# One engine fewer for the low halves: VectorE takes over GpSimd's weight pieces in the attention stages

## The chip, the cores and the metric

The kernel runs on one core of one Trainium2 chip. Times are device microseconds (us) of one execution. The time before is the median of three runs. The profile is of one further execution, whose own time is given beside its span. The engines are called TensorE (PE in the profile, with its weight loads as PEld), VectorE (DVE), ScalarE (ACT), GpSimd (POOL) and SyncE (SP); SPq is SyncE's queue, from which all DMAs of this kernel are issued in program order.

## The reference, cut to what matters

Two layers of a hybrid attention block (each with a global attention A, a neighbourhood attention B, and gates), then one block of feed-forward, mixer, feed-forward and embedding stages, all on 272 or 256 tokens with 1024 channels in float32.

```python
proj = jnp.einsum('bld,de->ble', rms_norm(x, norm_g), w_in)
qa, ka, va, za, qb, kb, vb, zb, ga, gb = split_cols(proj)
oa = gqa_attention(rope(qa), rope(ka), va) * jax.nn.silu(za)
ob = neighbourhood_attention(qb, kb, vb, rpb) * jax.nn.silu(zb)   # scores + bias from rpb
mixed = jax.nn.sigmoid(ga) * (oa @ w_o_attn) + jax.nn.sigmoid(gb) * (ob @ w_o_na)
x = x + mixed @ w_out
```

`rpb` is the relative bias of attention B: it is gathered into a tile for each pair of heads and each tile of 128 queries.

## The kernel before, in words

**Weights in two halves.** A float32 product is made from three products of reduced-precision halves: x_hi·w_hi, x_lo·w_hi and x_hi·w_lo. The weights come as units, one DMA each. A unit of a layer has 16 blocks of 128 x 128 (1 MB). It lands in one of 3 `raw` buffers, ScalarE makes `w_hi` of it in one instruction of 128 x 2048 (`cut_to`, L798), and `w_lo = raw - w_hi` is made in 4 pieces of 128 x 512. `w_hi` and `w_lo` have 3 buffers each too. TensorE then multiplies its lines (L1946): a line is one output tile of 128 channels, 8 blocks and 24 matmuls. A unit has two such lines. The units of `ya` and `yb` have four lines of 4 blocks and 12 matmuls.

**Who makes w_lo.** `by_pool(u)` says whether the unit's name stands in `POOLS`. If it does, GpSimd makes the four pieces (L781). It does nothing else in these stages, so it makes them as soon as `w_hi` is there. If not, VectorE makes them (`lo_to`, L1227), in an order written out by hand: after it has read line g of the program out of PSUM, `lo_after` makes all pieces up to those that line g + 3 needs. Both raise a semaphore of their own, `lo_pool` or `lo_cut`. TensorE waits for it ahead of a line. SyncE waits for the last piece of unit u - 3 before it issues the load of unit u into the same `raw` buffer:

```python
if u >= RAW:
    sp.wait_ge(lo_pool if by_pool(u - RAW) else lo_cut, MADE[LO_END[u - RAW] - 1])
sp.dma_start(raw[:, u % RAW, 0:n], weights[u, :, 0:n]).then_inc(raw_in[u % RAW], 16)
```

**The attention stage of a layer.** It is a list of jobs, one per step t. ("A", c, half, t) and ("B", c, half, t) are scores of one head for 128 queries; layer 0 has 35 jobs (three of them for the 16 meta tokens), layer 1 has 32. The products that need no attention result are used as fillers between them: za (4 lines), zb (4), ga (8), gb (8), and last ya (8). Some steps have no filler: 3, 7 and 11 in layer 1, and 3, 7, 11, 15, 19 and 23 in layer 0. At step t TensorE does: scores(t), the filler's line, the turn (transpose of the probabilities) of job t-1, the values of job t-2, and, every other step, the transpose of a finished pair. VectorE does at step t: maxes(t), the filler's evacuation (L1286, L1447), the normalization of job t-2 (L1435, L1436), then `lo_after`, then the rest. ScalarE does exps(t), `cut_to` of the unit two after the filler's, the gate's tanh, and the copy of the turn of job t-1.

**The bias tiles.** The 8 bias tiles of a layer (numbered 0 to 7) share 4 `rel` buffers. `window_bias(k)` (L1376) is VectorE's first use of tile k, ahead of the maxes of a step. It waits for `rel_in`, that is for the tile's four DMAs (L700). The first four tiles are loaded early. Tiles 4 to 7 are issued by SyncE right behind a weight load:

```python
for n in range(RING, len(BIASES)):
    if u == rel_unit(i, n):
        load_rel(i, n)
```

`rel_unit` gives, in units counted from the layer's first: layer 0, tiles 4 and 5 behind the load of unit 22, 6 behind 23, 7 behind 24; layer 1, tile 4 behind 21, 5 behind 22, 6 behind 23, 7 behind 24. The load of unit 22 waits for the last low piece of unit 19, and so on. VectorE needs them at these steps: layer 0, tiles 4, 5, 6, 7 at steps 25, 27, 29, 31; layer 1 at steps 22, 24, 26, 28. Units 17 to 20 are the lines of gb, 21 and 22 those of ya, 23 and 24 those of yb.

Of the kernel before, what the change touches and what calls it, by code (L numbers as in the profile page):

```python
# [139 lines left out]

POOLS = {"za", "zb", "ga", "gb", "ya", "gv", "iq", "gr", "ms", "yg"}


def by_pool(u):

    return UNITS[u][0][1] in POOLS

# [2348 lines left out]
```

## Time and profile before

| what | value |
|---|---|
| median of 3 runs | 1212.04 us (1210.35 to 1213.66) |
| the profiled execution: time, span | 1213.4 us, 1211.6 us |
| TensorE matmul busy | 1157.0 us, 95% |
| VectorE busy | 841.1 us, 69% |
| ScalarE busy | 602.8 us, 50% |
| GpSimd busy | 263.1 us, 22% |
| HBM read | 185.50 MB |

The busy shares are averages over stages. TensorE is at work nearly all the time; each us in which it stands still, or works at the lower of its two clocks, is close to a us of the kernel's time. Outside the span lie 1.8 us of the execution's time.

### The profile page before, as it was taken

The page shows a single profiled execution, that of the slowest core. Times are in us where ns is not written, and L with a number is a line of the kernel's source. Part 1 is how long each engine was busy: PE and PEld are TensorE (multiplying, and loading weights), DVE is VectorE, ACT ScalarE, POOL GpSimd, SP SyncE. Part 2 cuts the span into 40 slices and gives each one's busy share as a digit, 9 for nine tenths or more (in the row PEclk, how much of TensorE's full clock was granted, in tenths as well). Part 3 has the DMA queues.
Part 4 walks back from the last instruction along what each step waited for, and adds up shares of the span by engine and source line. Part 5 has one row for each costly group of instructions (what it writes and reads, how often), then busy time and mean ns, then how long its engine had stood idle before and what let it go on. Part 6 is the DMA issues. An engine that isn't in the chain of part 4 may idle for free.

```text
span 1211.6 us, 23199 instructions
## 1 busy us (share of the span) xinstructions
PE 1157.0 (95%) x9292; PEld 1126.0 (93%) x9292; DVE 841.1 (69%) x1823; ACT 602.8 (50%) x940; POOL 263.1 (22%) x199
## 2 busy tenths in 40 slices
PE   6999999899999999999999989999999999999995
PEld 6989999899899998899999988888899999999995
DVE  6954444879444468787766789677855887777666
ACT  6454545453555546544444533565454564444453
POOL 1055543000655600000000058800372000000000
PEclk9999999999999999999999999999999999999998
DMA  6752343356523624555455533325454555554551
GB/s 239 181 193 106 105 126 85 140 175 166 182 105 109 168 73 174 192 201 183 168 178 180 207 140 105 140 71 168 159 134 150 177 182 194 188 176 166 191 199 35
DMA packets 47979, 188.07 MB, mean 155 GB/s; under 512 B 20856, under 2 KB 24184, under 8 KB 29312
## 3 DMA queue, kind: packets, MB, share of 16 engines
q1 hardware_dynamic: 47872, 186.58, 46.2%
q8 instruction: 75, 1.23, 0.4%
q14 instruction: 32, 0.26, 0.1%
HBM read 185.50 MB, written 1.06 MB: 154 GB/s over the span
## 4 chain that ended last, share of the span: by engine, by line
PE 76%; DVE 15%; ACT 4%; issue 2%; DMA 2%; POOL 0%; SPq 0%; DVEq 0%; ACTq 0%
PE line L1946 48%; PE result L1946 17%; DVE w_lo L1227 4%; PE turn L2072 1%; PE result L2106 1%; PE stat L2106 1%; PE score L2049 1%; ACT w_hi L798 1%; PE score L2053 1%; DMA raw<-in_weights 1%; DMA rel<-in_rpb 1%; PE score L2238 1%; DVE prod L1792 1%; DVE prod L1503 0%; DVE root L1249 0%
## 5 line engine op out<-in xcount | busy, mean ns | idle before, releaser
L781 POOL TENSOR_TENSOR w_lo<-raw,w_hi 128x512 fp32r<-128x512 f32 x184 | 258.9, 1439 | 592.0 <-ACT w_hi L798 591.9
L798 ACT ACTIVATE w_hi<-raw 128x2048 fp32r<-128x2048 f32 (+2 forms) x178 | 321.8, 1809 | 113.9 <-PE line L1946 42.3
L1946 PE MATMUL line<-x_hi,w_hi 128*128 128x256 f32 (+1 forms) x1144 | 339.1, 296 | 17.6 <-DVE x_lo L1270 8.6
L1227 DVE TENSOR_TENSOR w_lo<-raw,w_hi 128x512 fp32r<-128x512 f32 (+2 forms) x528 | 324.8, 660 | 5.5 <-ACT w_hi L798 3.0
L1946 PE MATMUL line<-x_hi,w_lo 128*128 128x256 f32 (+1 forms) x1144 | 327.1, 286 | 0.0
L1946 PE MATMUL line<-x_lo,w_hi 128*128 128x256 f32 (+1 forms) x1144 | 326.6, 285 | 0.0
L1946 PEld LDWEIGHTS line<-x_hi,w_hi 128*128 128x128 f32 x1144 | 218.5, 191 | 24.5 <-issue 16.5
L1946 PEld LDWEIGHTS line<-x_lo,w_hi 128*128 128x128 f32 x1144 | 217.9, 191 | 1.6
L1946 PEld LDWEIGHTS line<-x_hi,w_lo 128*128 128x128 f32 x1144 | 218.4, 191 | 0.0
L1946 PE MATMUL line<-y_hi,w_hi 128*128 128x256 f32 (+1 forms) x688 | 205.5, 299 | 3.6 <-DVE y_lo L1278 1.7
L1946 PE MATMUL line<-y_hi,w_lo 128*128 128x256 f32 (+1 forms) x688 | 196.0, 285 | 0.0
L1946 PE MATMUL line<-y_lo,w_hi 128*128 128x256 f32 (+1 forms) x688 | 195.6, 284 | 0.0
L1946 PEld LDWEIGHTS line<-y_hi,w_hi 128*128 128x128 f32 x688 | 131.3, 191 | 6.2 <-DVE y_lo L1278 2.1
L1946 PEld LDWEIGHTS line<-y_lo,w_hi 128*128 128x128 f32 x688 | 131.0, 190 | 1.6
L1946 PEld LDWEIGHTS line<-y_hi,w_lo 128*128 128x128 f32 x688 | 131.4, 191 | 0.0
L1946 PE MATMUL result<-x_hi,w_hi 128*128 128x256 f32 (+1 forms) x232 | 65.5, 282 | 0.0
L1946 PE MATMUL result<-x_lo,w_hi 128*128 128x256 f32 (+1 forms) x232 | 65.4, 282 | 0.0
L1946 PE MATMUL result<-x_hi,w_lo 128*128 128x256 f32 (+1 forms) x232 | 65.4, 282 | 0.0
L924 ACT ACTIVATE probs<-score,top 128x272 f32<-128x272 f32 (+1 forms) x66 | 32.2, 488 | 65.8 <-DVE top L1397 35.7
L1946 PE MATMUL result<-y_lo,w_hi 128*128 128x256 f32 x192 | 54.0, 281 | 0.0
L1946 PE MATMUL result<-y_hi,w_lo 128*128 128x256 f32 x192 | 54.0, 281 | 0.0
L1946 PE MATMUL result<-y_hi,w_hi 128*128 128x256 f32 x192 | 53.9, 281 | 0.0
(323 smaller groups left out, 2107.1 us busy)
## 6 DMA issues: line engine op xcount, KB each, us to landing
raw<-in_weights SPq DMA_DIRECT2D x145, 1024.0 KB, 4.9
raw<-in_weights SPq DMA_DIRECT2D x32, 704.0 KB, 4.0
rel<-in_rpb SPq DMA_DIRECT2D x64, 64.0 KB, 6.4
h<-in_tokens SPq DMA_DIRECT2D x2, 544.0 KB, 6.1
raw<-in_weights SPq DMA_DIRECT2D x2, 512.0 KB, 5.7
rbias<-bias_by_distance SPq DMA_DIRECT2D x8, 128.0 KB, 5.5
out<-wide SPq DMA_DIRECT2D x4, 256.0 KB, 2.2
consts<-in_consts SPq DMA_DIRECT2D x1, 832.0 KB, 6.7
```

Of the source, the lines that this page charges most:

```text
L781: pool.tensor_tensor(w_lo[:, u % CUT, at], raw[:, u % RAW, at], w_hi[:, u % CUT, at].bitcast(F32), ALU.subtract).then_inc(lo_pool, 1)
L798: act.activation(w_hi[:, v % CUT, first:n], raw[:, v % RAW, first:n], ACT.Copy).then_inc(hi_cut, 1)
L924: act.activation(probs[0:m, place % 2, half * SECOND:half * SECOND + TOK], score_bank[s % 2][0:m, 0:TOK], ACT.Exp, bias=top[0:m, n % 2, 0: ...
L1227: dve.tensor_tensor(w_lo[:, u % CUT, at], raw[:, u % RAW, at], w_hi[:, u % CUT, at].bitcast(F32), ALU.subtract).then_inc(lo_cut, 1)
L1792: link(dve.match_replace(work[:, t, 0:keys], best[:, :], src, TAKEN))
L1946: ins = pe.matmul(bank[:, 0:n], stay, move[:, first + k, 0:n], start=(k, m) == (0, 0), stop=(k, m) == (depth - 1, 2))
L2049: ins = pe.matmul(s[:, 0:TOK], qa[:, c, t * P:(t + 1) * P], ka_half[:, half * TOK:(half + 1) * TOK], start=True, stop=True)
L2053: ins = pe.matmul(s[:, 0:TOK], qb[:, c, t * P:(t + 1) * P], kb[:, c, half * TOK:(half + 1) * TOK], start=True, stop=True)
L2072: ins = pe.transpose(turn_bank[:, b * P:b * P + m], probs[0:m, place, first:first + P], ident[0:m, 0:m])
L2106: ins = pe.matmul(single_bank[pair % 2][:, cols], tn[:, b * P:(b + 1) * P], v[:, kt, cols], start=(half, kt) == (0, 0), stop=b == both)
L2238: ins = pe.matmul(bank[:, g * P:(g + 1) * P], keys[:, at], queries, start=True, stop=True)
```

## The change

The five names of the layers' units leave `POOLS`. The 14 units per layer of za, zb, ga, gb and ya, 56 pieces per layer and 112 in all, are then made by VectorE at `lo_after`, where it skipped them before. TensorE and SyncE wait for `lo_cut` in place of `lo_pool` for these units, and the counts in `MADE` follow from the same table. GpSimd keeps the 18 units of the mixer. Everything else stays.

```diff
-POOLS = {"za", "zb", "ga", "gb", "ya", "gv", "iq", "gr", "ms", "yg"}
+POOLS = {"gv", "iq", "gr", "ms", "yg"}
```

## Rows read from the trace of the kernel before

**Rows 1.** Windows, A and B steps: busy (count) PE, PEld, DVE, ACT, POOL; PEclk, DMA, GB/s.

```profile
84.00:193.00 109.00, 107.40 (x849) 101.27 (x848) 48.43 (x121) 54.75 (x121) 59.23 (x47) 1.00 0.37 115
...
323.00:424.00 101.00, 100.53 (x814) 97.54 (x814) 47.16 (x110) 55.30 (x117) 62.89 (x47) 1.00 0.41 125
```

**Rows 2.** Groups by form: low pieces on GpSimd (64 to 200 us), on VectorE (215 to 290 us).

```profile
L781 POOL TENSOR_TENSOR w_lo<-raw,w_hi 128x512 fp32r<-128x512 f32 x56 | 74.3, 1360 | 115.3 <-ACT w_hi L798 115.3
...
L1227 DVE TENSOR_TENSOR w_lo<-raw,w_hi 128x512 fp32r<-128x512 f32 x43 | 27.8, 683 | 0.1
```

**Rows 3.** Timeline, layer 0, steps 21 to 25: GpSimd, SyncE's queue, VectorE.

```profile
160.50 5.00 POOL L781 TENSOR_TENSOR w_lo<-raw,w_hi 128x512 fp32r<-128x512 f32 x4 [5.90 <-ACT w_hi L798]
...
165.52 0.33 SPq L685 DMA_DIRECT2D raw<-in_weights  x1
165.90 6.77 SPq L700 DMA_DIRECT2D rel<-in_rpb  x8
...
171.34 0.29 DVE L1436 TENSOR_TENSOR head_out<-result,share 128x128 f32<-128x128 f32 x1
...
176.83 0.69 DVE L1376 TENSOR_TENSOR rel<-rel,consts 128x512 f32<-128x512 f32 x1 [5.20 <-DMA rel<-in_rpb]
```

**Rows 4.** Chain that ended last, 178 to 180 us: start, us, what.

```profile
178.45 0.42 ACT gate_b L961
...
179.40 0.41 PE turn L2072 x2
```

**Rows 5.** Layer 0, tile 7: loads, time to landing, VectorE's step 30; TensorE's turn, from the chain.

```profile
186.85 0.33 SPq L685 DMA_DIRECT2D raw<-in_weights  x1
...
L700 SPq DMA_DIRECT2D rel<-in_rpb x4: 616/622/982, 187.2 to 189.6; - x4
...
DMA to landing us min/median/max: 5.5/5.8/6.1
...
196.67 0.29 DVE L1436 TENSOR_TENSOR head_out<-stat,share 128x128 f32<-128x128 f32 x1
...
201.13 0.22 PE turn L2072 x2
```

**Rows 6.** Layer 1, tile 7: the same views, step 27.

```profile
416.71 0.33 SPq L685 DMA_DIRECT2D raw<-in_weights  x1
...
L700 SPq DMA_DIRECT2D rel<-in_rpb x4: 595/616/617, 417.1 to 419.0; - x4
...
DMA to landing us min/median/max: 5.7/6.4/6.9
...
427.45 0.29 DVE L1436 TENSOR_TENSOR head_out<-stat,share 128x128 f32<-128x128 f32 x1
...
431.75 0.22 PE turn L2072 x2
```

**Rows 7.** Tiles loaded further ahead: layer 1, tile 4 (steps 19, 22, 23); layer 0, tile 6.

```profile
395.49 0.29 DVE L1436 TENSOR_TENSOR head_out<-stat,share 128x128 f32<-128x128 f32 x1
404.04 0.98 DVE L1376 TENSOR_TENSOR rel<-rel,consts 128x512 f32<-128x512 f32 x1
...
410.98 0.22 PE turn L2072 x2
...
189.70 0.70 DVE L1376 TENSOR_TENSOR rel<-rel,consts 128x512 f32<-128x512 f32 x1
...
195.47 0.22 PE turn L2072 x2
```

**Rows 8.** TensorE after a standstill: timeline, then two windows (columns as in the first group).

```profile
711.29 0.36 PE L1946 MATMUL line<-x_hi,w_hi 128*128 128x256 f32 x1 [3.26 <-DVE wide L1287]
...
711.00:714.00 3.00, 2.71 (x15) 2.74 (x16) 2.96 (x4) 0.00 (x0) 3.00 (x3) 0.67 0.94 397
714.00:717.00 3.00, 3.00 (x22) 3.00 (x21) 0.74 (x2) 0.86 (x2) 2.36 (x2) 0.77 0.11 40
```

**Rows 9.** Timeline: one VectorE form while GpSimd works.

```profile
150.45 1.75 DVE L1376 TENSOR_TENSOR rel<-rel,consts 128x512 f32<-128x512 f32 x1
```

## The prediction, made before the changed kernel was built

> **What bounds the kernel now.** I read the page first: TensorE is busy 95% of the span, the others far less. So an edit can only help where TensorE stands still, and only hurts where it makes TensorE stand still. Then the windows of the two attention stages, where the whole edit lies. There the reader is to see how full TensorE is: 107.40 of 109.00 us in layer 0's A and B steps, 100.53 of 101.00 in layer 1's [rows 1]. The two stretches have 1.60 + 0.47 = 2.07 us of standstill. VectorE is busy for 48.43 and 47.16 us of them, under half, and GpSimd for 59.23 and 62.89. Last I read who waits for the low pieces. TensorE never does in these steps. SyncE does: it holds each weight load back until the last low piece of the unit three before is made, and the bias tiles 4 to 7 of a layer are issued behind such loads. VectorE itself waits for such a tile once today: tile 4 of layer 0, 5.20 us [rows 3]. So the place to look at is not VectorE's busy share but the time at which the last piece of a unit is made.
>
> **Part 1, work that moves.** 112 pieces leave GpSimd, 1.36 us each [rows 2]. On VectorE a piece is 27.8 / 43 = 0.65 us where GpSimd is idle, two are 1.29 us. Per layer that is 56 x 0.65 = 36 us more on VectorE. In the two stretches GpSimd makes 47 pieces each [rows 1], 47 x 0.65 = 30.6 us: VectorE would be busy 48.43 + 30.6 = 79 of 109 us and 47.16 + 30.6 = 78 of 101. It stays below TensorE. The pieces are made three lines ahead, so TensorE doesn't wait for them either: a piece slips by at most some us against three lines of about 3 us, each with its attention work between. The scores of step t are used by TensorE one whole step later (turn t comes behind the line of step t+1), which covers 1.29 us more ahead of maxes. At the few steps ahead of one without a filler this cover is thin, since ScalarE cuts a unit between the exps and the copy of a turn; I take up to 0.4 us at each of five, 1 us in all. Without the cover it would be 5 x 1.29 = 6.5 us. Cost of part 1: 1 us, from 0 to 6.5.
>
> **Part 2, VectorE and GpSimd no longer slow each other.** The window tile's addition, 0.69 us alone [rows 3], took 1.75 us while GpSimd worked [rows 9]. Such excess goes. But what it can give is bounded by TensorE's standstill in these stages, 2.07 us [rows 1], and most of that follows other chains. I take 1 us, from 0 to 2.1. The Trainium skill (SBUF — State Buffer, Who interferes with whom) says that a VectorE instruction with two SBUF inputs and a GpSimd one that reads SBUF exclude each other for the whole of an instruction. The trace agrees in kind (1.75 against 0.69 us). By that rule alone the edit is a gain, and by the windows that gain would be at most 2.1 us.
>
> **Part 3, the last piece of a unit is made later, and loads queue behind it.** GpSimd makes the four pieces as soon as `w_hi` is there. VectorE makes them in halves, by its written order: for a unit of two lines u, the first half at the second line of u-2, the other half at the first line of u-1. For unit 21 (ya, the line order takes one piece at a time) the last piece comes at step 30 in layer 0 and step 27 in layer 1, behind the first line of ya. Set beside the steps at which VectorE asks for the tiles, that gives eight cases:
>
> - Layer 0: tiles 4 and 5 can be issued only behind step 24, where unit 19 is finished. Tile 4 is asked for at the head of step 25, at once. Tile 5 at 27. Tile 6 behind step 26, asked at 29. Tile 7 behind step 30, asked at step 31, at once.
> - Layer 1: tile 4 behind step 19, asked at 22; 5 behind 21, asked at 24; 6 behind 23, asked at 26. Tile 7 behind step 27, asked at 28, at once.
>
> In the three cases "at once" VectorE waits for a whole weight load and four tile DMAs. It doesn't deadlock: the piece is made ahead of the wait. Behind the waiting instruction on VectorE stand the maxes of that step, and behind these ScalarE's exps and TensorE's turn; TensorE has one more step of work, then stands still. The other five cases have two or more steps.
>
> *Tile 4, layer 0.* Today GpSimd ends unit 19 at 160.50 + 5.00 = 165.50, the load is issued at 165.52, the tile lands at 176.8, 11.3 us behind it (eight tile DMAs are in that batch), and the turn that hangs on it starts at 179.40, behind the wait [rows 3, 4]. So here all slack is used already. Changed: the normalization of step 24 ends at 171.34 + 0.29 = 171.63, two pieces more make 172.92. That is 172.92 - 165.50 = 7.4 us later, and the turn 7.4 us later: 7.4 us of standstill. If the tile lands 8.9 us behind the load, as in the batches of four DMAs below, it is 5.0.
>
> *Tile 7, layer 0.* Load to landing today: last issue 189.6, at most 6.1 to land, less 186.85 = 8.9 us [rows 5]. Changed, on today's clock: 196.67 + 0.29 + 0.65 = 197.6, landing 206.5. From tile to turn it takes 179.40 - 176.83 = 2.57 us in the case above, less 0.42 for the gate's tanh, which ya has not: 2.15 [rows 3, 4]. The turn starts at 208.6 in place of 201.13 [rows 5]: 7.5 us.
>
> *Tile 7, layer 1.* Load to landing 419.0 + 6.9 - 416.71 = 9.2 us [rows 6]. Changed: 427.45 + 0.29 + 0.65 = 428.4, landing 437.6, turn 439.7 in place of 431.75: 8.0 us. For both tiles 7 I keep as bounds 5 us (landing 3 us sooner: 5.5 to 5.8 us is what single tile DMAs take) and 10 us (11.3 to land).
>
> *The other five.* Tile 4 of layer 1: pieces done at 395.49 + 0.29 + 1.29 = 397.1, landing 406.3, asked for at 404.04 [rows 7]. VectorE waits 2.2 us; the turn could start at 406.3 + 2.57 = 408.8 and is due at 410.98. Nothing lost, 2.1 us to spare. Tile 6 of layer 0 is the tightest, since VectorE has a backlog behind the first stall. It is due, 7.4 us later than today, at 197.1 for the bias, and the turn at 202.9 [rows 7]. I place its load at 190.6 (landing of tile 4 at 184.2, then two evacuations, two maxes, a normalization, four pieces), landing 199.5, turn 202.1: 0.8 us to spare. Taken at nothing; at 11.3 us to land it would cost 1.6.
>
> **Part 4, the clock behind each standstill.** After TensorE had stood still for 3.26 us, its granted clock was 0.67 and 0.77 in the next two windows of 3 us, so it worked at 1.2 GHz for part of them: (0.33 + 0.23) x 3 = 1.7 us lost [rows 8]. The three stalls are 7 to 8 us each. 3 x 1.7 = 5.1 us, bounds 0 and 6. The Trainium skill (TensorE: Matmul & The Clock Gate, What's actually happening) says that the throttled state is the default and that activity releases it. The trace agrees, with the 0.67 and 0.77 behind a wait. If the clock weren't touched, the sum would be 5.1 us less.
>
> **Sum.** 1.0 - 1.0 + 7.4 + 7.5 + 8.0 + 0 + 5.1 = 28.0 us. The profiled execution took 1213.4 us (span 1211.6), so 1241.4 for such a one; it lies 1.4 us above the median of the runs, 1212.04, which gives 1240.0.
>
> **Rivals.**
>
> *The moved work is hidden; no change, or the small gain of part 2.* This is the one on the other side. For it: VectorE is idle over half of the stage, and TensorE has not waited for pieces. It decides if the tiles land soon after the load is issued: for tile 4 of layer 0 within 176.83 - 172.92 = 3.9 us, where it was 11.3 and the fastest single tile DMA of [rows 5, 6] took 5.5 alone. The time would be 1212.0 - 2.1 to 1212.0: 1210 to 1212. Chance 0.05, for an error of mine in the order of issue.
>
> *Only the first of the stalls counts.* If tile 7's DMAs land sooner because the DMA engines are nearly idle in the ya steps, or VectorE reaches unit 21 sooner than I read, then 7.4 + 1.7 and a few us remain: 1221 to 1227. Against it: the four issues themselves take 2.4 us and the landing row is from that very place. Chance 0.12.
>
> *VectorE becomes the bound.* Backlogs behind the stalls, the thin cover of part 1 (6.5), and the tiles that I take as in time (1.6 in each of four, and a clock lost with some) add 10 to 15 us: 1250 to 1256. For it: 0.8 us is a thin margin, and at 78 of 101 us VectorE has little to catch up with. Chance 0.15.
>
> *The forecast,* three stalls and nothing else: 1240, its own range 1230 to 1248. Chance 0.68.
>
> **Range and chances.** 1225 to 1252 holds the forecast's case, the better part of the second rival's upper end and the third's lower end. 0.3% of this kernel, 3.6 us, is about what its measurement can tell from no change. Faster by more needs a gain that the 2.07 us of standstill can't give: 0.02. Within: 0.04. Slower: 0.94.
>
> **What the profile would show.** Right: VectorE's `rel` (L1376) waits for the DMA three times, each some 8 to 11 us, at step 25 and 31 of layer 0 and step 28 of layer 1; TensorE stands still 7 to 8 us behind each, with a granted clock under 1 behind it; the load of unit 22 is issued right behind two VectorE pieces; pieces of about 0.68 us, none slowed; all stages from the first feed-forward block on as long as before. Wrong: TensorE waiting for `w_lo` itself, VectorE busy without a gap through the gate lines, more than three long `rel` waits, or none.

## The result and the profile after

The changed kernel takes 1246.58 us (median of 4 runs, 1245.49 to 1248.51), the kernel before 1212.15 on the same chip (4 runs, 1210.35 to 1213.66). The ratio is 1.0286, 95% interval 1.0267 to 1.0306: slower by 34.4 us. Forecast were 1240.0 and a range of 1225 to 1252. The profiled execution took 1245.87 us, its span is 1244.1 us, 32.5 us longer than the span before.

The page of the changed kernel, busy time by engine: TensorE has the same number of matmuls and 7 us more of busy time, VectorE only 39 us more.

```profile
PE 1164.2 (94%) x9292; PEld 1131.7 (91%) x9292; DVE 880.4 (71%) x1935; ACT 600.8 (48%) x940; POOL 113.2 (9%) x87
```

The same windows of the A and B steps as in [rows 1], then four windows of 3 us from inside the first standstill on. The columns are those of [rows 1].

```profile
84.00:193.00 109.00, 98.96 (x764) 92.84 (x764) 59.13 (x150) 50.19 (x113) 0.00 (x0) 0.95 0.32 103
323.00:424.00 101.00, 97.06 (x767) 93.81 (x766) 59.74 (x140) 52.02 (x111) 0.00 (x0) 0.98 0.36 128
183.00:186.00 3.00, 0.00 (x0) 0.00 (x0) 0.72 (x2) 0.00 (x0) 0.00 (x0) 0.50 0.49 68
186.00:189.00 3.00, 1.15 (x6) 1.19 (x7) 2.93 (x9) 1.61 (x5) 0.00 (x0) 0.50 0.00 0
189.00:192.00 3.00, 3.00 (x13) 2.77 (x13) 2.07 (x5) 2.95 (x6) 0.00 (x0) 0.50 0.00 0
192.00:195.00 3.00, 3.00 (x25) 3.00 (x24) 1.00 (x5) 0.58 (x2) 0.00 (x0) 0.92 0.71 243
```

In layer 0 TensorE lost 107.40 - 98.96 = 8.4 us of busy time in 109 us, and VectorE is still busy only 54% of it. So VectorE isn't the bound: TensorE stands still for something that also leaves VectorE idle. The timeline of layer 0, steps 24 and 25 (answers to [rows 3]), shows it:

```profile
172.40 0.29 DVE L1436 TENSOR_TENSOR head_out<-result,share 128x128 f32<-128x128 f32 x1
172.62 1.29 DVE L1227 TENSOR_TENSOR w_lo<-raw,w_hi 128x512 fp32r<-128x512 f32 x2
...
173.94 0.33 SPq L685 DMA_DIRECT2D raw<-in_weights  x1
...
174.31 6.34 SPq L700 DMA_DIRECT2D rel<-in_rpb  x8
...
185.28 0.69 DVE L1376 TENSOR_TENSOR rel<-rel,consts 128x512 f32<-128x512 f32 x1 [11.37 <-DMA rel<-in_rpb]
```

The load of unit 22 is issued at 173.94, 0.03 us behind the end of two VectorE pieces (before: 165.52, behind GpSimd's). The eight tile DMAs follow it in the queue, and VectorE waits 11.37 us for tile 4. The chain that ended last says the same, and what comes behind (start, us, what):

```profile
172.69 1.23 DVE w_lo L1227 x2
174.31 0.60 SPq L700
...
176.27 8.99 DMA rel<-in_rpb
187.85 0.66 PE turn L2072 x2
...
190.69 3.87 PE line L1946 x24
...
195.87 3.02 PE line L1946 x24
```

The turn that started at 179.40 starts at 187.85. The line behind it takes 3.87 us where the next takes 3.02. The granted clock is 0.50 in three windows above, then 0.92; experiment 9 shows that the difference is the clock. The two tiles 7 look the same. Timeline, layer 0 step 30 and 31, then layer 1 step 27 and 28 (answers to [rows 5, 6]):

```profile
207.47 0.68 DVE L1227 TENSOR_TENSOR w_lo<-raw,w_hi 128x512 fp32r<-128x512 f32 x1
...
208.18 0.33 SPq L685 DMA_DIRECT2D raw<-in_weights  x1
...
208.56 2.57 SPq L700 DMA_DIRECT2D rel<-in_rpb  x4
...
216.75 0.69 DVE L1376 TENSOR_TENSOR rel<-rel,consts 128x512 f32<-128x512 f32 x1 [8.60 <-DMA rel<-in_rpb]
...
449.97 0.33 SPq L685 DMA_DIRECT2D raw<-in_weights  x1
...
458.74 0.69 DVE L1376 TENSOR_TENSOR rel<-rel,consts 128x512 f32<-128x512 f32 x1 [8.79 <-DMA rel<-in_rpb]
```

The waits over both attention stages (engine, line, waited for: us in total, times, longest). The first group is the changed kernel's, 60 to 480 us:

```profile
DVE rel L1376 <- DMA rel<-in_rpb: 31.3, 6, 11.4
PE turn L2072 <- ACT turned L944: 26.7, 8, 8.0
```

The second is that of the kernel before, 60 to 460 us:

```profile
PE turn L2072 <- ACT turned L944: 1.6, 5, 0.6
```

**Where the 32.5 us are.** Both programs give TensorE the same 9292 matmuls in the same order, so I paired them and read how far each starts behind its partner. In the attention stages the distance grows at these places and hardly anywhere else:

| place | us |
|---|---|
| four steps ahead of one without a filler | 0.25 + 0.81 + 0.64 + 0.98 = 2.7 |
| three standstills, tile 4 and 7 of layer 0, tile 7 of layer 1 | 7.39 + 7.44 + 7.79 = 22.6 |
| the line behind each, at the lower clock | 2.15 + 1.99 + 2.16 = 6.3 |
| sum at the end of layer 1's attention | 31.6 |

From there on the distance isn't constant: 30.1 us at 478 to 690 us of the kernel before, 32.7 at 727, 32.2 at the last matmul (32.5 in the span). The stretches at the lower clock outside the attention stages fall differently in the two executions. The kernel before has one at 462.8 us, the changed kernel a longer one at 742. The medians differ by 2 us more than the spans: the profiled execution of the kernel before was 1.3 us slower than its median, that of the changed kernel 0.7 us faster. I can't say more of those 2 us.

### The profile page after: what moved, and what is told of

The parts are those of the page before. It is cut to its first block, busy times and chain, and to the rows that moved or that the text cites. A ratio compares the mean times of both kernels' runs of the same rounds, so it can differ in the third digit from the quotient of the medians.

```text
span 1244.1 us, 23199 instructions
## 1 busy us (share of the span) xinstructions
PE 1164.2 (94%) x9292; PEld 1131.7 (91%) x9292; DVE 880.4 (71%) x1935; ACT 600.8 (48%) x940; POOL 113.2 (9%) x87
## 4 chain that ended last, share of the span: by engine, by line
PE 74%; DVE 16%; ACT 4%; issue 3%; DMA 2%; SPq 1%; DVEq 0%; ACTq 0%
PE line L1946 46%; PE result L1946 17%; DVE w_lo L1227 5%; DMA rel<-in_rpb 2%; PE turn L2072 1%; PE result L2106 1%; PE stat L2106 1%; ACT w_hi L798 1%; PE score L2053 1%; PE score L2049 1%; DMA raw<-in_weights 1%; PE score L2238 1%; DVE prod L1792 1%; DVE prod L1503 0%; DVE root L1249 0%
## 5 line engine op out<-in xcount | busy, mean ns | idle before, releaser
L1227 DVE TENSOR_TENSOR w_lo<-raw,w_hi 128x512 fp32r<-128x512 f32 (+2 forms) x640 | 391.8, 657 | 5.8 <-ACT w_hi L798 3.0
L781 POOL TENSOR_TENSOR w_lo<-raw,w_hi 128x512 fp32r<-128x512 f32 x72 | 109.0, 1545 | 323.6 <-ACT w_hi L798 323.6
L924 ACT ACTIVATE probs<-score,top 128x272 f32<-128x272 f32 (+1 forms) x66 | 32.2, 487 | 112.9 <-DVE top L1397 73.5
L2072 PE MATMUL turn<-consts,probs 128*128 128x128 f32 (+1 forms) x166 | 29.7, 278 | 26.8 <-ACT turned L944 26.7
```

The lines of the kernel that those rows point to most:

```text
L781: pool.tensor_tensor(w_lo[:, u % CUT, at], raw[:, u % RAW, at], w_hi[:, u % CUT, at].bitcast(F32), ALU.subtract).then_inc(lo_pool, 1)
L924: act.activation(probs[0:m, place % 2, half * SECOND:half * SECOND + TOK], score_bank[s % 2][0:m, 0:TOK], ACT.Exp, bias=top[0:m, n % 2, 0: ...
L1227: dve.tensor_tensor(w_lo[:, u % CUT, at], raw[:, u % RAW, at], w_hi[:, u % CUT, at].bitcast(F32), ALU.subtract).then_inc(lo_cut, 1)
L2072: ins = pe.transpose(turn_bank[:, b * P:b * P + m], probs[0:m, place, first:first + P], ident[0:m, 0:m])
```

## The experiments

Ten runs of eight kernels, in three groups. The kernel before took 1212.87, 1213.24 and 1213.38 us beside them; each ratio is against the kernel before of the same group. The groups ran on different chips, so a difference between groups is given also with each kernel set against the kernel before of its own group.

**1. Take the tiles out from behind the late load.** The changed kernel, with one edit in SyncE's program: the tiles are issued ahead of the weight load, so that they no longer wait for the last low piece. `load_rel` still waits until its buffer's former tile has been used.

```diff
 for u in range(1, NU):
+    for i in range(DEPTH):
+        for n in range(RING, len(BIASES)):
+            if u == rel_unit(i, n):
+                load_rel(i, n)
     load_unit(u)
...
-        for n in range(RING, len(BIASES)):
-            if u == rel_unit(i, n):
-                load_rel(i, n)
```

> VectorE makes all the pieces as in the changed kernel, but SyncE issues tiles 4 to 7 ahead of the weight load that they stood behind, so that they no longer wait for that load's last low piece. Theory (loads queued behind a late last piece): the three long waits for the tiles go, and with them the 22.1 us of stall and 6.6 us of lower clock that the trace after shows; what is left is 2.8 us of the thin covers at the steps without a filler, so about 1215 us (1213 to 1218). Rival (VectorE is the bound or its backlog makes the stalls): the waits change owner and the time stays above 1235. Second rival (the tile DMAs themselves are slow wherever they stand): 1225 to 1240.

Measured: 1213.99 us (12 runs), ratio 1.0008 (0.9992 to 1.0025). No wait for `rel` is left in the trace, and TensorE's long standstills are gone. 1246.58 - 1213.99 = 32.6 us (33.3 when each is set against the kernel before beside it) hung on the place of 32 DMAs of 64 KB (tiles 4 to 7 of both layers) behind weight loads. TensorE's lag at the steps ahead of one without a filler is still there.

**2. The same edit on the kernel before**, to see whether it is worth something by itself.

> The kernel before (GpSimd makes the pieces of the gate lines) with the same edit of SyncE's order. Theory: the 5.20 us wait for tile 4 of layer 0 goes, which cost TensorE about 0.6 us; 1211.4 us, the same as before within the measurement. Rival (the order of the loads is worth much by itself): below 1208. The difference to the run with VectorE making the pieces is the price of the moved work alone: 2.8 us by the theory.

Measured: 1210.29 us (12 runs), ratio 0.998 (0.9965 to 0.9996). The wait of [rows 3] cost the kernel before 0.73 us of TensorE's time by the pairing. So the price of the moved work alone, with tiles ahead on both sides, is 1213.99 - 1210.29 = 3.7 us, 2.8 expected. Each of the two ratios is good to about 2 us, and the pairing gives 2.7.

**3. GpSimd keeps the three units** whose last piece gates the tiles that are asked for at once (19 and 21 of layer 0, 21 of layer 1); all the others move.

```diff
-    return UNITS[u][0][1] in POOLS
+    return UNITS[u][0][1] in POOLS or UNITS[u][0] in (
+        ("layer0", "gb", 4), ("layer0", "ya", 0), ("layer1", "ya", 0))
```

> The changed kernel, but three of the 28 units are made by GpSimd again: unit 19 of layer 0 (gb 4, 5) and unit 21 of both layers (ya 0 to 3), those whose last piece gates a tile that VectorE asks for at once. 100 of 112 pieces stay on VectorE. Theory: the three stalls go, tile 4 of layer 0 waits 5 us as before; about 1215 us (1213 to 1219). Rival (VectorE's load): 12 of 112 pieces less is 11% of the loss of 34 us, so above 1240.

Measured: 1221.06 us (6 runs), ratio 1.0062 (1.0041 to 1.0084), 6 us above what I expected and 2 above its range. Tile 7 of both layers is in time, but there are five waits for `rel`, 18.6 us together. The longest is for tile 6 of layer 1, which I had taken as in time. Timeline of this kernel:

```profile
419.32 0.33 SPq L685 DMA_DIRECT2D raw<-in_weights  x1
...
419.70 3.34 SPq L700 DMA_DIRECT2D rel<-in_rpb  x4
...
423.61 0.33 SPq L685 DMA_DIRECT2D raw<-in_weights  x1
...
423.98 5.79 SPq L700 DMA_DIRECT2D rel<-in_rpb  x4
...
431.67 0.69 DVE L1376 TENSOR_TENSOR rel<-rel,consts 128x512 f32<-128x512 f32 x1 [6.31 <-DMA rel<-in_rpb]
```

Tile 6 landed 431.67 - 419.32 = 12.3 us behind its load, where batches alone took 8.6 and 8.8 us above. GpSimd ends the pieces of unit 21 early, so the next load and its four tile DMAs are issued 4.3 us behind, while tile 6 is still on its way. That this is why it landed late is argued from the rows here and in experiment 4; no run changed it alone. TensorE stood still for 3.58 us there, and for 1.02 and 0.54 us at two tiles of layer 0. With 1.6 us at the lower clock behind the 3.58, and the lag of 2.7, this is 9.4 us. The pairing has 9.1 at the end, the medians 8.2.

**4. Only these three units move:** the kernel before, with 12 of the 112 pieces on VectorE.

```diff
-    return UNITS[u][0][1] in POOLS
+    return UNITS[u][0][1] in POOLS and UNITS[u][0] not in (
+        ("layer0", "gb", 4), ("layer0", "ya", 0), ("layer1", "ya", 0))
```

> The kernel before, but VectorE makes just those three units, 12 pieces, and GpSimd keeps the other 100. Theory: all three stalls come, with the lower clock behind each: 22.1 + 6.6 = 28.7 us, so about 1240 us (1236 to 1244). Rival (VectorE's load): 12 of 112 pieces are 3.7 us, about 1216. A result of 22 us, 1234, would say that the clock term is not real.

Measured: 1248.04 us (4 runs), ratio 1.0289 (1.0266 to 1.0312). Expected were 1240 and a range of 1236 to 1244, so it came out 8 us above what I expected. Twelve pieces cost as much as 112. At tile 4 of layer 0 one reason is that GpSimd still works beside them: the timeline of this kernel shows the two pieces of unit 19 at 2.39 us (1.29 in the changed kernel), beside GpSimd's four of the next unit:

```profile
173.43 2.39 DVE L1227 TENSOR_TENSOR w_lo<-raw,w_hi 128x512 fp32r<-128x512 f32 x2
...
173.56 5.88 POOL L781 TENSOR_TENSOR w_lo<-raw,w_hi 128x512 fp32r<-128x512 f32 x4 [17.09 <-ACT w_hi L798]
...
175.85 0.33 SPq L685 DMA_DIRECT2D raw<-in_weights  x1
...
187.80 0.69 DVE L1376 TENSOR_TENSOR rel<-rel,consts 128x512 f32<-128x512 f32 x1 [11.98 <-DMA rel<-in_rpb]
```

Its waits in both stages are three, and long:

```profile
DVE rel L1376 <- DMA rel<-in_rpb: 34.2, 3, 12.0
```

TensorE's standstills are 9.08, 9.26 and 10.54 us, with 1.7 to 2.5 us of clock behind each. At the two tiles 7 the last piece isn't slowed (0.68 us). There the tile lands later behind its load: 10.6 us in layer 0, 11.5 in layer 1, against 8.6 and 8.8 in the changed kernel, and that is nearly the whole difference of the standstills (9.26 against 7.44, 10.54 against 7.79). GpSimd has made the next unit early, and the next load is issued 3.0 us behind the first, where in the changed kernel none follows for 20 us. Timelines of layer 1:

```profile
450.16 0.33 SPq L685 DMA_DIRECT2D raw<-in_weights  x1
...
453.16 0.60 SPq L685 DMA_DIRECT2D raw<-in_weights  x1
...
461.69 0.69 DVE L1376 TENSOR_TENSOR rel<-rel,consts 128x512 f32<-128x512 f32 x1 [11.55 <-DMA rel<-in_rpb]
```

**5. Where the 3.7 us of moved work are.** The kernel of experiment 1, with the pieces behind the next step's maxes instead of ahead of them.

```diff
             maxes(...); shares(...)      # of step t
+            if FILLER_AT[i].get(t - 1) is not None:
+                lo_after(name, *FILLERS[FILLER_AT[i][t - 1]])
...
-            if f is not None:
-                lo_after(name, *FILLERS[f])
-                if f:
-                    silu_of(f - 1)
+            if f:
+                silu_of(f - 1)
```

> Tiles issued ahead of the weight loads, and VectorE makes the pieces of a step behind the next step's maxes in place of ahead of them; GpSimd still makes none in the layers. Theory (the 2.7 us left are the two pieces ahead of the maxes, on the chain to ScalarE's cut and the copy of the turn, at the steps ahead of one without a filler): those 2.7 us go, about the time of the kernel before with tiles ahead, 1210 to 1211. Rival (VectorE has too much to do in these stages wherever the pieces stand): 1214 as with tiles ahead alone. Second rival (pieces now too late for TensorE or for the weight loads): 1216 or more, with waits for w_lo or raw.

Measured: 1210.01 us (12 runs), ratio 0.9966 (0.995 to 0.9981). TensorE's wait for the copied turn, ahead of the next turn, was 3.8 us in the kernel of experiment 1 (waits, 5 times, longest 1.1 us) and is 0.8 here, and by the pairing the lag at all four places is gone. The windows of this kernel, columns as before, and its row of pieces in the first window:

```profile
84.00:193.00 109.00, 108.19 (x855) 102.18 (x854) 64.88 (x165) 56.02 (x123) 0.00 (x0) 1.00 0.38 117
323.00:424.00 101.00, 100.52 (x814) 97.46 (x813) 64.13 (x161) 56.87 (x121) 0.00 (x0) 1.00 0.41 125
...
L1228 DVE TENSOR_TENSOR w_lo<-raw,w_hi 128x512 fp32r<-128x512 f32 x42 | 27.1, 683 | 0.0
```

TensorE is busy for 108.19 of 109.00 us in layer 0, 0.8 more than before. VectorE's other work takes 64.88 - 27.1 = 37.8 us, against 48.43 beside GpSimd.

The medians gained more than the 2.7 us of the pairing, 4.0 us (4.4 when each is set against the kernel before beside it). Part of that is something that I had not looked for. In every kernel of this document VectorE makes the pieces of `yb`, and at the end of a layer's attention one of them stands ahead of an evacuation that ScalarE and TensorE wait for. Timeline of the kernel before, layer 0:

```profile
214.19 0.68 DVE L1227 TENSOR_TENSOR w_lo<-raw,w_hi 128x512 fp32r<-128x512 f32 x1
214.79 0.42 DVE L1471 TENSOR_TENSOR wide<-result,silu_b 128x256 f32<-128x256 f32 x1
```

The edit puts that piece behind the evacuation too (213.17 and 213.50 in the trace of this kernel). TensorE's waits for the halves of its result (L1479) fall from 1.2 us in each layer to 0.6 and 0.7; the pairing shows 0.59 and 0.58 us.

**6. The same as 5 and 2, once more**, on another chip, since they stand close together.

> The kernel with tiles ahead and the pieces behind the maxes once more, beside the one in which GpSimd makes the pieces with tiles ahead, on one chip. Theory: the two are within 0.15% of each other, both 0.2 to 0.4% under the kernel before; the engine that makes the pieces is worth nothing once order is right. Rival (VectorE free of GpSimd's interference gains by itself): this one is 1 to 2 us faster than the other.

> GpSimd makes the pieces, tiles ahead, once more for that comparison: 1210 to 1211 us by the theory, 1 to 2 us slower than the other by the rival.

Measured: 1210.76 us (12 runs), ratio 0.9966 (0.9951 to 0.9981), and 1211.42 us (12 runs), ratio 0.9993 (0.9974 to 1.0012). The kernel of experiment 5 beats the one before by 0.34% both times. Whether it also beats the kernel before with its tiles ahead isn't settled: side by side 0.7 us lie between them, less than either's interval. Nor is it like with like: the reordering also moves the pieces of `yb`, which gives 0.59 and 0.57 us by the pairing in this run too. A kernel in which GpSimd keeps its pieces and only those of `yb` move was not run. So the 0.34% is the worth of both orders together, and says nothing for one engine against the other. I had expected both kernels 0.2 to 0.4% under the one before; with tiles ahead alone it was 0.20% the first time and 0.07% the second.

**7. One standstill alone:** the kernel of experiment 1, with tiles 4 and 5 of layer 0 behind the load of unit 22 again.

```diff
-            if u == rel_unit(i, n):
+            if u == rel_unit(i, n) and (i, n) not in ((0, 4), (0, 5)):
                 load_rel(i, n)
     load_unit(u)
+    for n in (4, 5):
+        if u == rel_unit(0, n):
+            load_rel(0, n)
```

> As with tiles ahead, but tiles 4 and 5 of layer 0 stand behind the load of unit 22 again. Theory: one stall of the three comes back, 7.4 us and 2.1 us of lower clock, so 1214.0 + 9.5 = 1223.5 us (1221 to 1226). Rival (the stalls feed each other, or one is mostly absorbed when the others are gone): within 3 us of 1214, or above 1230.

Measured: 1223.74 us (4 runs), ratio 1.0079 (1.005 to 1.0108), as expected. One wait of 10.93 us is left, a standstill of 6.94 us, and the line behind it takes 4.33 us. The lower clock costs 2.6 us here by the pairing. 1223.74 - 1213.99 = 9.8 us for one tile (9.4 when each is set against the kernel before beside it); the changed kernel has three such places.

**8. Is the rest the clock?** The changed kernel, with TensorE kept busy in the three standstills by matmuls of the identity into a bank that is free then (60 at each place). The layers and steps are (0,26), (0,32) and (1,29), ahead of the turn.

```diff
+if (i, t) in ((0, 26), (0, 32), (1, 29)):
+    for _ in range(60):
+        pe.matmul(single_bank[PAIRED[(i, jobs[t - 4])] % 2][:, 0:P],
+                  ident, ident, start=True, stop=True)
```

> The changed kernel; at the three stalls TensorE is given 60 matmuls of 128 columns whose results nobody reads (about 6.6 us, inside waits of 7.4 to 7.8 us), so it waits while at work. Nothing of the reference's computation is changed. Theory (each stall is followed by a stretch at 1.2 GHz that costs 2.1 us by the offsets of the trace): the granted clock stays at 1 behind them and 3 x 2.1 = 6.3 us come back, about 1240 us (1239 to 1243). Rival (the slower stretch is something else, such as VectorE's backlog): 1246 to 1248, and the lines behind the stalls still take 3.9 us in place of 3.0.

Measured: 1253.53 us (4 runs), ratio 1.0322 (1.0298 to 1.0346). This missed its aim. The chain of this kernel shows why:

```profile
181.83 13.40 PE result L2137 x120
```

Each matmul ran as two passes, so 60 took 13.4 us, not the 6.6 I had reckoned with, and ended 5.3 to 6.0 us behind where the wait had ended. The clock did stay at 1.00.

**9. The same with 29**, which take 6.64 us.

> As the busy wait before, but with 29 matmuls at each stall: each float32 one ran as two passes of 0.11 us, so 60 of them were 13.40 us and reached 6 us beyond the waits; 29 are 6.5 us and end inside them. Theory: granted clock 1 behind the stalls, the three stalls stay as long, and 3 x 2.1 = 6.3 us come back: 1240 us (1238.5 to 1242.5). Rival (the slow stretch is not worth anything in the end, or the waits themselves shrink or grow): 1246, or outside both.

Measured: 1237.11 us (4 runs), ratio 1.0189 (1.0161 to 1.0217), 9.5 us less than the changed kernel (10.7 when each is set against the kernel before beside it). That is a larger gain than forecast, which was 1240 us with a range of 1238.5 to 1242.5. Windows and chain of this kernel at the first standstill:

```profile
186.00:189.00 3.00, 1.90 (x18) 1.74 (x17) 2.63 (x7) 1.28 (x4) 0.00 (x0) 1.00 0.14 30
189.00:192.00 3.00, 3.00 (x24) 2.92 (x25) 2.86 (x9) 2.25 (x3) 0.00 (x0) 1.00 0.02 5
```

```profile
190.47 3.03 PE line L1946 x24
```

The standstills, now filled, are nearly as long as ever (7.00, 7.33, 7.73 us, 22.1 together, against 22.6), the clock is 1.00 and the line takes 3.03 us in place of 3.87. By the pairing the end lies 25.05 us behind the kernel before, where the changed kernel lies 32.2: 7.1 us less, of which the clock at the three places gives 6.2 (6.3 in the table, 0.1 left here) and the shorter standstills 0.5. The median gained 9.5. The remainder of 2.4 us, or 3.6 against the kernel before beside it, stays open.

## Why the prediction was right

**The mechanism and the three places: right.** SyncE's load behind the last low piece, tiles behind the load, VectorE's wait, TensorE's standstill. Experiment 1 removed it by moving the DMAs alone and 32.6 us went; experiment 7 put back two tiles, of which one made VectorE wait, and 9.8 us came back; experiment 4 made it out of twelve pieces. The rival "VectorE becomes the bound" falls with experiment 1, where VectorE has all the moved work and the kernel loses 1 us. "Only the first stall counts" falls with the two rows of tiles 7. The other side, no change, falls with the result.

**Part 3, 7.4 + 7.5 + 8.0 = 22.9 us: right.** 7.39, 7.44 and 7.79 measured. From load to landing it took 185.28 - 173.94 = 11.3 us for the batch of eight DMAs, and 8.6 and 8.8 us for those of four, against 11.3, 8.9 and 9.2 read from before. The five other tiles cost TensorE nothing, as forecast: VectorE waited three times, 1.5 us at most. But the margin was luckier than I wrote. Landing at a fixed distance behind the load was an assumption that experiments 3 and 4 broke: 12.3, 10.6 and 11.5 us with the next load 4.3, 3.0 and 3.0 us behind. In experiment 3 that cost 3.58 us. In the changed kernel the loads that tiles 4 to 7 stand behind are followed by the next one after 8.3 us at the least, since late pieces also keep the loads apart. I had not reckoned with that.

**Part 1, 1.0 us: too small.** 2.7 us by the pairing, 3.7 by experiments 1 and 2. I had allowed up to 0.4 us at each of five steps; four lost time, 0.25 to 0.98 us each. I had named ScalarE's cut between the exps and the copy of the turn, but I priced the cover of the maxes, one step of TensorE's work, and didn't add up the whole chain. At a step whose next has no filler, VectorE's two pieces come ahead of the rest of the evacuation and the next maxes. Behind these come the exps, then ScalarE's cut of a whole unit (1.90 us from 119.21), the gate's tanh and only then the copy of the turn. The chain that ended last of the changed kernel, layer 0, steps 9 and 10 (the turn was at 120.90 before and is 1.05 us later):

```profile
116.79 1.20 DVE w_lo L1227 x2
118.00 0.35 DVE silu_b L1459
118.35 0.36 DVE top L1402
...
119.31 0.90 ACT w_hi L798
...
121.01 0.42 ACT gate_a L961
121.43 0.39 ACT turned L944
...
121.95 0.41 PE turn L2072 x2
```

Experiment 5 shows it: the pieces behind the maxes, and the wait of 3.8 us falls to 0.8.

**Part 2, -1.0 us: nothing on the path.** The interference is gone: 10.6 us of VectorE's time in layer 0's window (experiment 5), so my forecast of 79 of 109 us busy was too high by as much as 14. None of it showed on the path of the changed kernel. The one stall that stood ahead of it, the 0.73 us behind tile 4 of layer 0, was replaced by the first standstill.

**Part 4, 5.1 us: right in kind, a little low.** 6.3 us, just above my upper bound of 6. The granted clock fell to 0.50, the lower of the two levels, already during the standstill, and stayed there past 192, over 4 us behind its end at 187.85. I had priced it by a standstill of 3.26 us [rows 8]; these are twice as long, but each cost only 0.4 us more. Experiment 9, with TensorE busy through the same waits, is the measurement of it. The Trainium skill (TensorE: Matmul & The Clock Gate, What's actually happening) says that activity releases the throttle; the traces agree, with 0.50 where TensorE stood still, 0.92 in the window from 192 on, and 1.00 behind the first standstill in experiment 9.

**The sum.** 28.0 us were forecast; by terms 2.7 + 0 + 22.6 + 6.3 = 31.6 were found, 32.5 in the span and 34.4 in the medians. Of the 6.4 us that the forecast lacked, 1.7 are part 1, 1.0 part 2 and 1.2 part 4, less 0.3 of part 3; 0.9 lie in the span behind the attention stages, and some 2 us no trace places.

## What to carry to other kernels

When work moves to an engine that is under half busy, don't ask how much it adds but when its last piece is done and what is queued behind that moment. Here a DMA queue in program order held 64 KB tiles, needed at once, behind a 1 MB load that was in no hurry but gated. Issue the small, urgent transfers ahead of the gated one, and put the moved pieces behind the instruction that the next engine waits for; then the move costs nothing here that the measurement can tell (1210.0 and 1210.8 us, against 1210.3 and 1211.4 with GpSimd's pieces and tiles ahead).

## What was not expected

- Twelve pieces (1248.04 us) cost as much as 112 (1246.58 us). The amount of work moved says nothing of the loss.
- A tile's landing seems to depend on what is issued behind it: 8.6 and 8.8 us behind its load when nothing followed for 20 us; 10.6, 11.5 and 12.3 when the next 1 MB load was issued 3.0, 3.0 and 4.3 us behind. No run changed this alone.
- With GpSimd silent VectorE's remaining work in 109 us shrank from 48.43 to 37.8 us. None of that showed in the time of the changed kernel.
- The clock's price hardly follows the length of the standstill: 1.6 us behind one of 3.58, 2.0 to 2.6 behind those of 6.9 to 7.8, 1.7 to 2.5 behind those of 9.1 to 10.5. Useless matmuls in the wait take that part away.
- One piece of 0.68 us ahead of the wrong evacuation had cost the kernel before 0.6 us in each layer.
- A float32 matmul of 128 x 128 was executed as two passes, 13.40 / 120 = 0.11 us each.
